# Joining the blocks of weight products into three longer ones, with two banks for the rotations

## What is computed

```python
for i in range(2):
    mix = sb_rwkv_mixer(...) if i == 0 else mla_mixer(...)      # ends in a product with hyb_out / mla_o
    h = h + mix
    h = h + conv_glu(rmsnorm(h, ffn_norm[i]), ffn_w_in[i], conv_w, conv_b, ffn_w_out[i])
    e = rmsnorm(p[i] @ ple_w_proj[i], ple_norm[i])
    gate = sigmoid(rmsnorm(h, ple_gate_norm[i]) @ ple_w_gate[i])
    h = h + gate * e
# mla_mixer: down = hn @ w_down, split in cq (384), ckv (256) and a rotated key part;
# q = rmsnorm(cq) @ w_uq with part of each head rotated; k, v = rmsnorm(ckv) @ w_ukv; causal softmax; @ w_o
```

## Time and profile before

| | us |
|---|---|
| runs (3): median | 2250.63 |
| runs: lowest, highest | 2249.33, 2266.69 |
| profiled execution | 2245.24 |
| its span, first to last instruction | 2243.3 |
| granted TensorE clock, mean share | 0.943 |

### The profile page before, as it was taken

One profiled execution on the slowest core, in us unless ns is written; L12 is line 12 of the kernel. 1 busy time (PEld: TensorE's weight loads), 2 busy tenths in 40 slices (PEclk: granted clock), 3 DMA queues, 4 the chain that ended last, 5 costly groups with the idle time before them and its releaser, 6 DMA issues. The chain is left out here.

```text
span 2243.3 us, 44055 instructions
## 1 busy us (share of the span) xinstructions
PE 1987.2 (89%) x15844; PEld 1916.9 (85%) x15844; DVE 1490.8 (66%) x3086; ACT 1232.5 (55%) x2435; POOL 0.2 (0%) x4
## 2 busy tenths in 40 slices
PE   6998878999999866999999896897998977899896
PEld 6887778999999855999999796897998977789896
DVE  4666555899744598666666577764677566467855
ACT  4454554777665599555555457102565543656644
POOL 0000000000000000000000000000000000000000
PEclk9999998999999999999999997987999988899999
DMA  5433433455555400455655351002464522156452
GB/s 179 144 99 99 126 100 123 141 178 171 180 185 185 158 0 0 153 194 194 191 195 191 118 186 50 1 2 69 159 194 159 178 94 85 39 157 195 157 182 66
DMA packets 96223, 295.96 MB, mean 132 GB/s; under 512 B 9315, under 2 KB 25830, under 8 KB 95974
## 3 DMA queue, kind: packets, MB, share of 16 engines
q1 hardware_dynamic: 96102, 294.35, 40.9%
HBM read 293.26 MB, written 1.05 MB: 131 GB/s over the span
## 5 line engine op out<-in xcount | busy, mean ns | idle before, releaser
L422 PE MATMUL bank<-a_high,w_high 128*128 128x256 f32 x3256 | 941.2, 289 | 118.7 <-DVE w_low L396 48.7
L396 DVE TENSOR_TENSOR w_low<-ring,w_high 128x512 fp32r<-128x512 f32 x1102 | 747.4, 689 | 435.0 <-ACT w_high L390 429.3
L390 ACT ACTIVATE w_high<-ring 128x512 fp32r<-128x512 f32 x1102 | 679.1, 628 | 455.2 <-PE bank L424 453.7
L423 PE MATMUL bank<-a_low,w_high 128*128 128x256 f32 x3256 | 924.1, 284 | 0.0
L424 PE MATMUL bank<-a_high,w_low 128*128 128x256 f32 x3256 | 923.4, 284 | 0.0
L422 PEld LDWEIGHTS bank<-a_high,w_high 128*128 128x128 f32 x3256 | 633.1, 194 | 134.5 <-issue 77.7
L424 PEld LDWEIGHTS bank<-a_high,w_low 128*128 128x128 f32 x3256 | 633.9, 195 | 0.0
L423 PEld LDWEIGHTS bank<-a_low,w_high 128*128 128x128 f32 x3256 | 633.0, 194 | 0.7
L422 PE MATMUL bank<-s_high,w_high 128*128 128x256 f32 x1024 | 282.8, 276 | 2.0 <-DVE s_low L2019 2.0
L424 PE MATMUL bank<-s_high,w_low 128*128 128x256 f32 x1024 | 282.7, 276 | 0.0
L423 PE MATMUL bank<-s_low,w_high 128*128 128x256 f32 x1024 | 282.7, 276 | 0.0
(11 more groups left out here) (341 smaller groups left out, 1951.8 us busy)
## 6 DMA issues: line engine op xcount, KB each, us to landing
ring<-in_stream SPq DMA_DIRECT2D x279, 512.0 KB, 3.5
ring<-in_peer_u SPq DMA_DIRECT2D x128, 512.0 KB, 3.4
ring<-in_peer_v SPq DMA_DIRECT2D x128, 512.0 KB, 3.4
ring<-in_stream SPq DMA_DIRECT2D x32, 256.0 KB, 3.2
x<-in_x SPq DMA_DIRECT2D x4, 256.0 KB, 5.2
arena<-in_mem SPq DMA_DIRECT2D x1, 1024.0 KB, 11.4
out<-x SPq DMA_DIRECT2D x4, 256.0 KB, 2.6
consts<-in_consts SPq DMA_DIRECT2D x1, 640.0 KB, 8.1
```

Of the source, the lines that this page charges most:

```text
L390: self.nc.scalar.activation(self.w_high[:, h % SLOTS, :], self.raw(h), ACT.Copy)\
L396: self.nc.vector.tensor_tensor(self.w_low[:, h % SLOTS, :], self.raw(h), self.w_high[:, h % SLOTS, :].bitcast(F32), ALU.subtract)\
L422: self.nc.tensor.matmul(to, lh, rh, start=start, stop=False, **more)
L423: self.nc.tensor.matmul(to, lh, rl, start=False, stop=False, **more)
```

## The change

`products` becomes `segment`, which makes the same lists but does not run them, and `run`, which puts several segments into one `Block`: TensorE and SyncE go through the segments in order, and the duties of all are sorted into one list. Inputs of a segment that come out of the one before carry the semaphore and the key of the duty that makes them (`ready`), so each chunk waits for its own part; their duties, and the squares that need the last of them, stand behind that key with the second number 5. Input chunks of neighbouring segments lie in different places (`bases`). `before.clear` and `before.join` wait for banks of the segment before. The last unit of a segment marked `followed` has its duties one half behind its end, where those with a norm had three.

Three groups of calls are joined: the branches, `w_out` and `mem_q`; `hyb_out` to `mla_uv`; `mla_o` to `ple_gate.1`. That removes eleven boundaries between blocks and the block with the add, which becomes one more VectorE operation for each part of `branch_b`. In the block with `mla_uq`, both norms' squares are made together, their sums follow each other, and the rotations use banks 7 and 6 in turn. Semaphores of other parts share names, so that the number of semaphores stays in bounds; that part of the diff, the bookkeeping of `Counter` and the re-indented engine functions are left out:

```diff
-    def products(self, jobs, gated=None, also=None, bring=None, after=None, whole=None, beside=None,
-                 gates=None, also_landed=None):
+    def products(self, jobs, **more):
+        self.run([self.segment(jobs, **more)])
+
+    def run(self, segments):
+
+        nc = self.nc
+        duties = [d + (s,) for s in segments for d in s.duties]
+        duties.sort(key=lambda d: d[:2])
+        with nc.Block(no_gpsimd_drain=True) as block:
+            @block.sync
+            def _(sp):
+                for s in segments:
+                    s.sp(sp)
+
+            @block.tensor
+            def _(pe):
+                for s in segments:
+                    s.pe(pe)
+
+            @block.scalar
+            def _(act):
+                for _, _, kind, what, s in duties:
+                    s.act(act, kind, what)
+
+            @block.vector
+            def _(dve):
+                for _, _, kind, what, s in duties:
+                    s.dve(dve, kind, what)
+
+    def segment(self, jobs, gated=None, also=None, bring=None, after=None, whole=None, beside=None,
+                gates=None, also_landed=None, turn=0, before=None, bases=None, followed=False):
...
 
-        norms = [(s, start + 1, unit) for s, _, _, start, unit in sources if isinstance(s, Normed)]
+        norms = [(s, start + 1, unit) for s, _, _, start, unit, _ in sources if isinstance(s, Normed)]
+        brief = beside is not None and units[0].chunks < DC
         if beside is not None and len(norms) > 1:
-            norms[1] = (norms[1][0], units[0].end + 2, 1)
+            norms[1] = (norms[1][0], norms[0][1], 0) if brief else (
+                norms[1][0], units[0].end + 2, 1)
...
+        if brief:
+            squared[1] = self.hn[:, norms[0][0].chunks:DC, :]
+        spun_in = [7, 6] if brief else [7]
...
-                bank = len(room) % (6 if norms else 8)
+                bank = len(room) % (6 if norms or before is not None else 8)
...
-        for source, at, chunks, start, _ in sources:
-
-            duties += [(max(start - AHEAD, s0) + c // HALF, 0, "input", (source, c, at + c))
-                       for c in range(chunks)]
+        for source, at, chunks, start, _, slot in sources:
+            first_key = start - AHEAD if before is not None else max(start - AHEAD, s0)
+            keys = source.keys if isinstance(source, (Normed, Held, Later)) else ()
+            for c in range(chunks):
+                key = first_key + c // HALF, 0
+                if keys:
+                    key = max(key, (keys[c], 5))
+                duties.append(key + ("input", (source, c, slot + c)))
         for i, (_, start, u) in enumerate(norms):
-            duties += [(start, 2, "squares", i), (units[u].end + (1 if units[u].chunks == DC or not i else 3), 2, "root", i)]
+            known = (max(start, norms[i][0].keys[-1]), 5) if norms[i][0].keys else (start, 2)
+            duties += [known + ("squares", i), (units[u].end + 1, 2, "root", i)]
...
-            late = 1 if normed(u) is None or u >= joins else 3
+            late = 1 if normed(u) is None or u >= joins or followed and u == len(units) - 1 else 3
             for phase in range(5 if gated is not None else 0):
                 duties.append((unit.end + late + phase, 3, "gated", (u, phase)))
+                done_by[u, 0] = done_by[u, 1] = unit.end + late + phase
...
+        def clear_bank(pe, bank):
+
+            if bank not in latest and before is not None:
+                before.clear(pe, bank)
+            if bank in latest:
+                u, h = latest[bank]
+                for e in range(2):
+                    if gated is not None and e or gated is None and touches(u, h, e):
+                        pe.wait_ge(copied[e].sem, copied[e].at(copies(u, h, e)))
+
...
+            def clear(u, h):
+
+                if before is not None and prior[u, h] is None:
+                    before.clear(pe, room[u, h])
...
+            def swing(u, h):
+
+                pe.wait_ge(copied[0].sem, copied[0].at(copies(u, h, 0)))
+                n = swings(u, h)
+                pe.wait_ge(mean.sem, mean.at(min(n + 1, len(spun_in))))
+                if n >= len(spun_in):
+                    pe.wait_ge(swayed.sem, swayed.at(n - len(spun_in) + 1))
+                for i in range(2):
+                    ins = nc.tensor.matmul(self.bank[spun_in[n % len(spun_in)]][:, i * T:(i + 1) * T],
+                                           units[u].place.rot, raw(u, h)[:, i, :],
+                                           start=True, stop=True)
+                ins.then_inc(swung.up(), 1)
...
+                        pe.wait_ge(squares.sem, squares.at(i + 1))
+                        if before is not None:
+                            before.join(pe)
+                        if i and norm is not also and not brief:
+                            pe.wait_ge(mean.sem, mean.at(i))
...
+                    elif isinstance(source, Later):
+                        act.wait_ge(*source.ready[c])
...
+                if onto(u):
+                    sofar = units[u].place.onto(units[u].tile + 2 * h, 2)
+                    dve.wait_ge(copied[1].sem, copied[1].at(copies(u, h, 1)))
+                    nc.vector.tensor_tensor(sofar, sofar, to, ALU.add).then_inc(added.up(), 1)
...
-        with nc.Block(no_gpsimd_drain=True) as block:
-            @block.vector
-            def _(dve):
-                nc.vector.tensor_tensor(mixed, mixed, both, ALU.add)
-        self.products([("w_out", "fm", mixed, None)])
-        self.memory(kmem, vm)
+        onto = lambda n, c: mixed[:, n:n + c, :]
+        a = self.segment([("branch_a", "fm", oa, Times(onto, lambda n, c: gates[:, n:n + c, :], 0)),
...
+        b = self.segment([("w_out", "fm", Later(mixed, *a.ready("branch_b")), None)], turn=1,
+                         before=a, bases=[DC], followed=True)
+        self.memory(kmem, vm, a, b)
...
+        x_after = lambda gain, s, name: Normed(self.x, gain, DC, D, *s.ready(name))
+        a = self.segment([(f"ffn_in.{l}", "fm", x_after(f"ffn_norm_2.{l}", first, name), None)],
+                         gated=Ffn(gated, gate, conv, [f"ffn_conv_w_2.{l}.{k}" for k in range(3)],
+                                   f"ffn_conv_b_2.{l}"),
+                         bring=(self.at(PLE_AT, 2), self.dram[f"ple_{l}"]), turn=1, before=first,
+                         followed=True)
+        b = self.segment([(f"ffn_out.{l}", "fm", Later(gated, *a.ready(f"ffn_in.{l}")), None)],
+                         turn=2, before=a, bases=[DC], followed=True)
         p, e, gate = self.at(PLE_AT, 2), self.at(PLE_AT + 2 * T, 8), self.at(PLE_AT + 10 * T, 8)
...
+        c = self.segment([(f"ple_proj.{l}", "fm", Held(p, self.fetched.sem, self.fetched.total + 16),
+                           lambda n, c: e[:, n:n + c, :]),
+                          (f"ple_gate.{l}", "fm",
+                           x_after(f"ple_gate_norm_2.{l}", b, f"ffn_out.{l}"),
+                           Applied(lambda n, c: gate[:, n:n + c, :], e, f"ple_norm_2.{l}", self.x))],
+                         also=Normed(e, f"ple_norm_2.{l}"), turn=3, before=b, bases=[DC + FC, 0],
+                         followed=True)
+        return [first, a, b, c]
...
-        self.products([("mla_down", "fm", Normed(x, "attn_norm_2.1"), lambda n, c: down[:, n:n + c, :])])
-        cq = Normed(down[:, 0:3, :], "mla_q_norm_2", 3, 384)
-        ckv = Normed(down[:, 3:5, :], "mla_kv_norm_2", 2, 256)
+        a = self.segment([("mla_down", "fm",
+                           Normed(x, "attn_norm_2.1", DC, D, *segments[-1].ready("ple_gate.0")),
+                           lambda n, c: down[:, n:n + c, :])], turn=4, before=segments[-1],
+                         bases=[DC], followed=True)
+        got, keys = a.ready("mla_down")
+        cq = Normed(down[:, 0:3, :], "mla_q_norm_2", 3, 384, got[0:3], keys[0:3])
...
+        b = self.segment([("mla_uq", "fm", cq, turned),
+                          ("mla_uk", "fm", ckv, Upper(lambda n, c: k[0:64, n:n + c, :], 64)),
+                          ("mla_uv", "tm", ckv, lambda h, n, c: v[:, h, n * P:(n + c) * P])],
+                         beside=beside, turn=5, before=a, bases=[2 * DC, 2 * DC + 3])
+        self.run([*segments, a, b])
...
-            k.hybrid()
-        for l in range(2):
-            if l:
-                with k.room(70 * T, DC):
-                    k.mla()
-            with k.room(50 * T, FC):
-                k.ffn(l)
-                k.ple(l)
+            out = k.hybrid()
+        with k.room(70 * T, DC + FC + 2):
+            first = k.segment([("hyb_out", "fm", out, None)], bases=[DC], followed=True)
+            out = k.mla(k.ffn(0, first, "hyb_out"))
+            first = k.segment([("mla_o", "fm", out, None)], bases=[DC], followed=True)
+            k.run(k.ffn(1, first, "mla_o"))
         with k.room(2 * T):
             k.finish()
```

787 lines of the change are left out of this document (400 added, 387 removed).

## The result

| | us | ratio to the kernel before (95%) |
|---|---|---|
| changed kernel, median of 4 runs | 2228.99 (2213.84 to 2235.29) | 0.989 (0.985 to 0.993) |
| kernel before beside it, median of 4 | 2258.66 | |
| changed kernel again, second comparison, 6 runs | 2220.89 (2213.55 to 2228.81) | 0.986 (0.982 to 0.989) |
| kernel before in that comparison, 11 runs | 2251.44 | |
| profiled execution after, its span | 2223.03, 2221.3 | |

The change makes the kernel faster by 1.1 to 1.4%, that is 24.6 us (15 to 34) in the first comparison and 32.4 us (24 to 41) in the second. The two profiled executions differ by 22.2 us. The forecast was 34.0 us. So the direction is as forecast.

The account below looks back on a forecast made before the run. TensorE was busy for 89% of the span, so gains had to come from its idle or slow stretches. Seven terms, 7.0 + 1.6 + 2.8 + 6.4 + 4.2 + 1.1 + 10.9 = 34.0 us, took 2250.63 to 2216.6 us (range 2205 to 2229).

## What to carry to other kernels

When blocks are joined, the barrier's time doesn't come back as such: each early piece of the next stage now stands in an in-order queue ahead of something more urgent, so walk every part of the stage before, not its last one, and then order the merged list by who waits (here that was worth 20 us more, as much as the joins, which alone gave 15.7). Work that hangs on a late result, and long work whose result is wanted late, goes behind what TensorE needs next. And before a difference of 1% between two executions is explained, the pace and the clock of the stretches that both share are to be compared: here the pace alone moved by 4%, and half clock added 7 us to a piece that no edit touched. Counting half clock needs the granted clock beside the distances, since of 219 distances of 215 to 245 ns in the trace before, 207 stand at 1.00 (146 of them in the products whose matmuls are 512 columns wide).
